# Moving the second half of the memory values from inside the attention loop to ahead of it

## The reference

```
h += W_o [ RMSNorm_a(DilatedSWA(group A)) ; RMSNorm_b(MLA(group B)) ]
h += CrossAttn(RMSNorm(h), RMSNorm(mem))      # 4 heads of 256, 256 memory tokens
h += MoE(RMSNorm(h))                          # top 4 of 32 experts, clamped SwiGLU
```

```
kv = (rmsnorm(mem, g_mem) @ w_mkv).reshape(b, m, 2, N_HEADS_MEM, HEAD_DIM_MEM)
k, v = kv[:, :, 0], kv[:, :, 1]
```

## Time and profile before

| | before |
|---|---|
| median of 3 runs | 1286.86 us |
| the profiled execution | 1287.3 us |
| its span in the trace | 1285.7 us |
| mean granted TensorE clock | 0.986 of full speed |
| TensorE busy | 1173.3 us, 91% |
| VectorE busy | 304.9 us, 24% |
| ScalarE busy | 205.3 us, 16% |
| DMA moved | 439.81 MB, 342 GB/s over the span |

### The profile page before, as it was taken

One profiled execution on the slowest core, in us unless ns is written; L12 is line 12 of the kernel. 1 busy time (PEld: TensorE's weight loads), 2 busy tenths in 40 slices (PEclk: granted clock), 3 DMA queues, 4 the chain that ended last, 5 costly groups with the idle time before them and its releaser, 6 DMA issues.

```text
span 1285.7 us, 17729 instructions
## 1 busy us (share of the span) xinstructions
PE 1173.3 (91%) x6951; PEld 502.4 (39%) x6952; DVE 304.9 (24%) x726; ACT 205.3 (16%) x384; POOL 2.3 (0%) x5
## 2 busy tenths in 40 slices
PE   7999999999899999899999888988999999999885
PEld 3476544675333333333333333333333333333332
DVE  3326553244611112111111111121111121111112
ACT  2120353131211111111111111111111111111111
POOL 0000000000000000000000000000000000000000
PEclk9998899999899999999999999999999999999998
DMA  9700155530599999999999999999699999999994
GB/s 372 302 1 2 38 225 185 240 148 1 244 375 428 429 427 430 427 430 428 428 429 428 430 428 429 427 430 392 273 428 429 428 429 428 430 427 430 429 429 173
DMA packets 37173, 439.81 MB, mean 342 GB/s; under 512 B 5536, under 2 KB 5664, under 8 KB 11456
## 3 DMA queue, kind: packets, MB, share of 16 engines
q1 hardware_dynamic: 36144, 439.30, 81.2%
q10 hardware_dynamic: 1008, 0.21, 0.1%
HBM read 438.45 MB, written 1.05 MB: 342 GB/s over the span
## 4 chain that ended last, share of the span: by engine, by line
PE 46%; DMA 46%; DVE 5%; issue 1%; ACT 1%; DVEq 0%; SPq 0%; ACTq 0%
DMA ring<-in_w_gate_up 45%; PE bank L1306 17%; PE bank L1323 6%; PE bank L992 4%; PE bank L1022 2%; PE bank L1014 2%; PE bank L1178 2%; PE bank L1169 2%; PE bank L1234 2%; PE bank L1126 1%; PE bank L1105 1%; PE bank L1113 1%; DVE stage L724 1%; PE bank L1064 1%; DMA stage<-in_w_in 1%
## 5 line engine op out<-in xcount | busy, mean ns | idle before, releaser
L1306 PE MATMUL bank<-ring,stage 128*64 128x512 f32 x2112 | 468.7, 594 | 47.8 <-DMA ring<-in_w_gate_up 47.8
L1306 PEld LDWEIGHTS bank<-ring,stage 128*64 128x64 f32 x2112 | 145.0, 137 | 352.1 <-issue 248.1
L1323 PE MATMUL bank<-ring,stage 128*64 128x512 f32 x1056 | 236.7, 601 | 22.7 <-ACT stage L537 22.7
L1323 PEld LDWEIGHTS bank<-ring,stage 128*64 128x64 f32 x1056 | 73.5, 138 | 164.8 <-issue 134.2
L947 DVE TENSOR_SCALAR stage<-bank 128x512 f32<-128x512 f32 x33 | 22.8, 692 | 354.4 <-PE bank L1306 354.4
L534 ACT ACTIVATE stage<-stage 128x512 f32<-128x512 f32 x33 | 20.8, 630 | 486.3 <-DVE stage L947 486.3
L862 DVE CAST stage<-cst 96x64 bf16 (+1 forms) x34 | 6.5, 191 | 331.5 <-PE bank L1306 331.5
L1288 PE MATMUL bank<-stage 64*128 64x512 f32 x264 | 65.6, 615 | 0.7 <-ACT stage L543 0.7
L1279 PEld LDWEIGHTS bank<-stage 128*128 128x128 bf16 x1632 | 50.6, 99 | 30.0 <-issue 29.2
L992 PE MATMUL bank<-stage,nT 128*128 128x488 f32 x128 | 54.3, 587 | 8.3 <-DMA stage<-in_w_in 8.3
L541 ACT ACTIVATE stage<-bank 128x512 f32<-128x512 f32 x33 | 19.7, 597 | 240.0 <-PE bank L1323 240.0
(11 more groups left out here) (230 smaller groups left out, 761.1 us busy)
## 6 DMA issues: line engine op xcount, KB each, us to landing
ring<-in_w_gate_up SPq DMA_DIRECT2D x128, 2048.0 KB, 23.8
ring<-in_w_down SPq DMA_DIRECT2D x64, 2048.0 KB, 21.8
ring<-in_w_mkv SPq DMA_DIRECT2D x8, 1024.0 KB, 23.4
stage<-in_w_in SPq DMA_DIRECT2D x8, 976.0 KB, 17.1
ring<-in_w_o SPq DMA_DIRECT2D x1, 4096.0 KB, 12.9
ring<-in_w_mq SPq DMA_DIRECT2D x1, 4096.0 KB, 23.8
stage<-in_w_mo SPq DMA_DIRECT2D x1, 4096.0 KB, 13.2
nT<-in_xT SPq DMA_DIRECT2D x2, 512.0 KB, 7.7
```

Source lines behind the costliest of these rows:

```text
L1306: ins = mm(bank[n // 2][lo:lo + BLK, :], xgT[:, k * BLK:(k + 1) * BLK], up_rows(k)[:, n * 512:(n + 1) * 512], start=False, stop=(k == KC - 1))
L1323: ins = mm(bank[3][n * BLK:(n + 1) * BLK, :], lhs, down_rows(f)[:, n * 512:(n + 1) * 512], start=(f == 0), stop=(f == 7))
```

## The change

TensorE's call `mem_values_in(1, (4, 5))` leaves step 3 of the attention loop and stands between the transposes of keys and the first scores, behind a wait for two of the four key copies (banks 4 and 5 are then free). ScalarE's two copies of the result leave the loop as well and stand right after the four key copies, ahead of the first exponential. The amount of work is the same. The only instruction-level differences are the places and one more wait.

```
@@ ScalarE @@
             for j in range(4):
                 act.wait_ge(S["k96_mm"], j + 1)
                 act.activation(kT96[...], spl(bank[4 + j][0:DQB, :], 2), ACT.Copy).then_inc(S["k96_ready"], 1)
+            mem_values_out(2, 4)
+            mem_values_out(3, 5)
...
-                if u in (1, 2):
-                    mem_values_out(u + 1, u + 3)
@@ TensorE @@
+            pe.wait_ge(S["k96_ready"], 2)
+            mem_values_in(1, (4, 5))
...
             for i in range(NU + 10):
-                if i == 3:
-                    mem_values_in(1, (4, 5))
                 if i < NU:
                     scores(i)
```

## The result

The changed kernel takes 1304.24 us, the median of four timed runs (1302.81 to 1305.4), against 1287.08 us (1286.56 to 1287.59). The ratio is 1.0129, with a 95% interval of 1.0116 to 1.0142. It is slower by 17 us, where I had forecast 0.9 us: the time lies far above the upper end of my range, 1289.4.

A forecast was written before the change was run, and what follows sets the result against it. The kernel was taken as bound by an unbroken chain of TensorE's program, then expert weight loads, passing delays on to the end. The terms summed to +0.9 us on a 1286.86 us median: 1287.8 us, range 1286.2 to 1289.4.

The forecast's parts named there:

- A: The forecast itself: the change costs +0.9 us, 1287.8 us, own range +0.86 to +2.0 us; chance 0.70.
- step 6: Attention loop: unit 5 to unit 7 takes 3.38 us and cannot catch up, so a late start stays late.
- Step 1: Ahead of attention: the 0.93 us gap behind the key transposes goes; the new wait costs 0.05 us.
- Steps 2 and 3: Value matmuls keep 13.93 us; the pipeline fill comes into the open, score 5 starting 5.18 us after score 0.
- Step 4: ScalarE's 1.28 us table load, no longer hidden, makes the first exponential 0.23 us late; slack covers it, cost 0.
- rival C: Table load ahead of the first exponential costs twice its length, +1.2 us on top: 1289.0 us; chance 0.03.
- Step 5: Loads of `w_o` and `w_mq` beside attention: `w_o` issues about 1.9 us earlier, cost 0.
- Rival D: TensorE's clock falls in attention's exposed fill, adding 2.85 us: 1290.6 us; chance 0.10.

The follow-up runs named there:

- the second trace: The changed kernel, unedited, traced once more: 1302.41 us.
- warm_fill: Changed kernel plus two extra matmuls nobody reads (256 and 512 columns) in TensorE's waits in step 3 of the attention loop: 1288.59 us, ratio 1.0009.
- pe_only: Changed kernel with ScalarE's two copies put back behind the exponentials of units 1 and 2, TensorE's part kept: 1303.34 us, ratio 1.0122.
- act_only: Changed kernel with TensorE's value matmuls put back in step 3 of the loop, ScalarE's part kept: 1305.66 us, ratio 1.0137.
- fill_first: Changed kernel plus one extra matmul nobody reads, 256 columns, ahead of the scores of unit 3: 1303.55 us, ratio 1.0156.
- values_at_1: Kernel before the change with the value matmuls in step 1 of the attention loop in place of step 3: 1305.71 us, ratio 1.0136.
- warm_router: Kernel before the change plus five extra matmuls of 512 columns, read by nobody, in TensorE's waits for the router: 1285.56 us, ratio 0.9985.

## Why the prediction was wrong

The step that failed is the one that the sum does not have. All terms of A, and step 6 above all (3.38 us from unit 5 to unit 7, so that a late start "stays late" and no more), are durations at full clock, and the clock was put at no change. In the runs it fell behind the exposed fill. From score 5 to score 7 were then 5.43 us, and attention took 14.5 us more in the second trace, where the sum has 0.9. The terms that the sum does have came out nearly as forecast.

**Step 1, the gap ahead: right.** The values follow the transposes at once (139.32 and 139.31 in the chain), a gap of 0, where I took 0.05 us. (By the rows the second key copy ends at 138.78 + 1.02 = 139.80, not near 139.9; nothing hangs on it.)

**Steps 2 and 3, the block and the exposed fill: right, a little large.** The block took 13.9 us. The fill can be read in `warm_fill`, where the clock holds. Score 5 starts 5.13 us after score 0 there (159.39 and 154.26), where I had 5.18. Counted from the end of the transposes (140.41) it is 18.98 us; before it was 18.25. The difference is 0.73 us, where I had 0.91.

**Step 4, the table load: right.** ScalarE's timeline in the first trace after, in answer to the earlier trace rows:

```profile
153.26 0.60 ACT L387 ACTIVATE v_mem<-bank 128x512 f32<-128x512 f32 x1 [6.27 <-PE bank L1024]
153.68 0.58 SPq L283 DMA_DIRECT2D ring<-in_w_mq  x1
153.88 1.28 ACT L440 ACT_TABLE_LOAD   x1
...
155.17 0.51 ACT L440 ACTIVATE stage<-stage,stat 128x256 f32<-128x256 f32 x1
```

VectorE's first scaling of probabilities in the same trace:

```profile
156.39 0.34 DVE L764 TENSOR_SCALAR stage<-stage,stat 128x256 f32<-128x256 f32 x1
```

The load stands directly behind the last copy, and the exponential directly behind the load, with no drain between (SyncE's row between them is the load of `w_mq`). The first exponential starts 2.02 us after the first score, against 1.69 before, so it is 0.33 us late. VectorE starts to scale 3.24 us after the first score, against 3.21 before, so the slack took nearly all of it. In `pe_only` the load is hidden again, and nothing is won. The drain of about 1380 ns, for which the Trainium skill, page "ScalarE: Activation LUTs", section "What ACT_TABLE_LOAD costs", made me keep rival C, does not show in either place (153.88 + 1.28 to 155.17; 207.59 + 1.28 to 208.88).

**Step 5, the loads: right.** They went out earlier (153.25), and in `warm_fill` they run beside the start of attention with the clock at 1.00 and no loss.

**Step 6, a late start stays late: right at full clock only.** In `warm_fill` attention is 0.7 us longer (68.96 against 68.22 us from the end of the key transposes to the output projection), and the kernel 1.0 us slower (interval about -0.1 to +2.4 us). In the changed kernel itself the cycle of 3.38 us took 5.43. The shift at the end of attention is the shift at the end of the kernel, as I had assumed: behind it the traces take 1077.5 and 1077.3 us.

**Rival D is what happened**, and I had both its chance and its price too low.

The first is the chance, 0.10. I wrote that the rows of 318 to 322 us "speak against" a fall, since the clock was 1.00 with 1.72 of 4.00 us busy. But the very next row has the fall, to a mean of 0.58. In the first trace the clock was likewise still 1.00 in the sparse stretch and fell right after it. Read so, the two rows speak for a fall, since they show one behind sparse work. I read the first as a state that holds. The busy share itself I had about right, with half: from 154.2 to 158.3 us in the first trace TensorE was busy for 2.24 of 4.10 us, and in the same place of the second (155.7 to 159.8) for 2.23. That is the same kind of stretch as the 1.72 of 4.00 ahead of the fall in the kernel before. So the rows had the answer, and the error was in how I read them.

The second is the price, 2.85 us. I took it from one episode of dense work. It has to be taken from the stage in which the clock falls: how much longer does this stage take at the lower level, and for how long does it stay there? From the two traces: 6.4 us (7.1 less 0.7 for the fill) in 17 us of low clock, 13.8 in 34, so 0.4 us for each. And the return comes late. In the second trace of the changed kernel, `pe_only`, `act_only`, `fill_first` and `values_at_1` the first score of group B (96 rows in place of 64) starts at 190.79, 192.09, 193.86, 191.62 and 192.80, and the clock is back 2.0 to 3.6 us behind it. That the return has to do with group B is a regularity of these traces; it was not tested, and the first trace (back at 174.8, in group A) is an exception to it.

The range ended at 1289.4, and D's own number, 1290.6, lay outside it. With the price right D would have stood at about 1302, far from the other cases.

What stays open: 2.7 us of the median's 17.2. The second trace shows 14.5 in attention, and its execution, 1302.41, was faster than all others but the first; those reach 1305.4 and have no trace. Two things are large enough: where the key transposes end (139.3 to 142.4 us in the traces), and a first up projection at the lower clock. The latter stands in the trace of `values_at_1` (1306.32 us, mean granted clock 0.971), and the median's executions had 0.971 as well, where the second trace had 0.973. That is a hint and not shown. Why the first trace recovered early is open too, and so is what exactly about the fill makes the clock fall: the length of one wait, or how little TensorE did over the whole of it.

## What to carry to other kernels

Work that seems to stand without use in the middle of a latency-bound pipeline may be what keeps TensorE's clock up, as the value matmuls did here. Before moving it, ask not only which wait it covers, but what the clock does in that wait and whether the stage behind can get it back. When a stretch sits near a fall, price the fall as the whole stage at the lower level, 13.8 us here and not 2.85. In a table of stretches, read a granted clock together with what stands ahead of it. And where such a hole can't be closed, two matmuls that nobody reads are a cheap test, and may be a cheap cure: `warm_fill` shows the first, and `warm_router`, with 0.15% gained, the second.

## What was not expected of the hardware

The same loop of score, softmax and transpose ran for 30 us at 0.50 and, entered otherwise, for 47 us at 1.00, with TensorE busy for 100% and 94% of the time. A wait of 0.87 us behind 14 us of dense matmuls left the clock alone, and one of 1.20 us (with 0.61 us ahead of it, filled or not) did not. These were different kernels, and where between the two the change comes was not measured. At the lower level a stretch of this latency-bound loop takes about 1.6 times as long: from score 5 to score 7 were 3.38 us before; in the chain of the first trace two units at the lower clock, from score to score, are 5.43 us:

```profile
158.59 1.15 PE bank L1111 x2
...
164.02 1.15 PE bank L1111 x2
...
169.46 1.15 PE bank L1111 x2
```
